# The expert gather reads x in place, with a step of eight elements, instead of a permuted copy

## The reference

```python
def hier_moe(x, w_grp, b_grp, w_exp, b_exp, w_gate, w_up, w_down):
    grp_logits = (xt @ w_grp).astype(jnp.float32) + b_grp
    ...
    weights = p_g[:, None] * jax.nn.softmax(top_vals, axis=-1)
    expert_id = g_top[:, None] * EXPERTS_PER_GROUP + top_idx
    ...
    def run_block(args):
        tok, e = args
        xb = x_pad[tok]
        h = jax.nn.silu(xb @ w_gate[e]) * (xb @ w_up[e])
        return h @ w_down[e]
    ...
    y = jnp.sum(y_assign.reshape(T, TOP_K, D).astype(jnp.float32) * weights[..., None], axis=1)
```

## Time and profile before

| | us |
|---|---|
| median of 3 runs | 1726.51 |
| lowest to highest | 1726.4 to 1727.92 |
| span of the profiled execution | 1725.1 |
| PE busy | 1413.4 (82%) |
| DVE busy | 375.8 (22%) |
| ACT busy | 269.0 (16%) |

### The profile page before, as it was taken

The page is one execution under the profiler, slowest core; times in us unless marked ns, Lnnn a source line. Parts: engine busy times, 40 slices in busy tenths (PEclk is TensorE's granted clock), DMA queues, the critical chain, the costliest instruction groups (busy, mean ns, idle before and its releaser), DMA issues.

```text
span 1725.1 us, 24051 instructions
## 1 busy us (share of the span) xinstructions
PE 1413.4 (82%) x9475; PEld 900.4 (52%) x9475; DVE 375.8 (22%) x752; ACT 269.0 (16%) x409; POOL 22.8 (1%) x79
## 2 busy tenths in 40 slices
PE   7999999877777777767999999997777777686785
PEld 3678886444434343433457788844443434343442
DVE  3222011511111111112433110114111111111134
ACT  1211000211111111111113200003111111121110
POOL 1000000000000000000000000000000000000000
PEclk9999999998989999989999999999899999898898
DMA  9532444389999999996844234334999999999970
GB/s 322 177 123 98 149 149 148 146 335 421 421 422 421 422 422 422 422 422 278 302 159 147 98 122 147 131 148 172 421 421 422 422 422 421 422 422 422 422 282 32
DMA packets 105010, 503.66 MB, mean 292 GB/s; under 512 B 15042, under 2 KB 18036, under 8 KB 54900
## 3 DMA queue, kind: packets, MB, share of 16 engines
q1 hardware_dynamic: 104228, 500.70, 72.4%
q10 hardware_dynamic: 720, 2.11, 0.3%
HBM read 501.73 MB, written 1.05 MB: 291 GB/s over the span
## 4 chain that ended last, share of the span: by engine, by line
PE 61%; DMA 29%; DVE 3%; ACT 3%; issue 2%; SPq 0%; POOL 0%; DVEq 0%; ACTq 0%; POOLq 0%
DMA ring<-in_w_down 29%; PE ps L552 16%; PE ps L979 10%; PE ps L861 7%; PE ps L839 5%; PE ps L989 5%; PE ps L566 5%; PE ps L957 4%; PE ps L944 4%; PE ps L588 2%; ACT scratch L1159 2%; PE ps L602 1%; DMA scratch<-in_ln 1%; DVE xT L1255 1%; DVE x L1205 0%
## 5 line engine op out<-in xcount | busy, mean ns | idle before, releaser
L957 PE MATMUL ps<-ring,scratch 128*32 128x256 f32 x4096 | 243.4, 391 | 69.3 <-DMA ring<-in_w_up 46.5
L552 PE MATMUL ps<-xT,ring 128*128 128x256 f32 x1280 | 279.7, 379 | 0.0
L552 PEld LDWEIGHTS ps<-xT,ring 128*128 128x128 f32 x1280 | 242.7, 190 | 33.7 <-issue 1.1
L979 PE MATMUL ps<-ring,scratch 128*32 128x512 f32 x1024 | 166.1, 807 | 108.5 <-DMA ring<-in_w_down 105.6
L957 PEld LDWEIGHTS ps<-ring,scratch 128*32 128x32 f32 x4096 | 156.7, 113 | 148.2 <-issue 77.5
L1594 DVE TENSOR_TENSOR scratch<-scratch,ps 128x1024 f32<-128x1024 f32 x64 | 78.1, 1221 | 405.0 <-PE ps L989 405.0
L979 PEld LDWEIGHTS ps<-ring,scratch 128*32 128x32 f32 x1024 | 44.2, 141 | 212.8 <-issue 212.8
L989 PE MATMUL ps<-scratch 128*128 128x512 f32 x256 | 118.4, 605 | 36.9 <-ACT scratch L1159 36.9
L944 PEld LDWEIGHTS ps<-scratch 128*128 128x128 f32 x1024 | 120.1, 193 | 15.9 <-issue 15.6
L944 PE MATMUL ps<-scratch 128*128 128x128 f32 x1024 | 120.1, 276 | 0.0
L989 PEld LDWEIGHTS ps<-scratch 128*128 128x128 f32 x256 | 46.0, 189 | 112.7 <-ACT scratch L1159 66.8
(11 more groups left out here) (247 smaller groups left out, 842.9 us busy)
## 6 DMA issues: line engine op xcount, KB each, us to landing
ring<-in_w_gate SPq DMA_DIRECT2D x128, 1024.0 KB, 13.9
ring<-in_w_up SPq DMA_DIRECT2D x128, 1024.0 KB, 18.3
ring<-in_w_down SPq DMA_DIRECT2D x128, 1024.0 KB, 16.7
ring<-in_w_in SPq DMA_DIRECT2D x48, 1024.0 KB, 6.9
ring<-in_w_br SPq DMA_DIRECT2D x12, 1024.0 KB, 6.0
ring<-in_w_o SPq DMA_DIRECT2D x8, 1024.0 KB, 4.9
ring<-in_w_ple_gate SPq DMA_DIRECT2D x8, 1024.0 KB, 8.1
ring<-in_ln SPq DMA_DIRECT2D x6, 1024.0 KB, 13.8
```

The costliest lines, as they stand in the source:

```text
L552: ins = mm(out[:, m * SEQ:m * SEQ + SEQ], w[k // per][:, k % per, m * 128:m * 128 + 128], rhs[:, k, :], start=(k == 0), stop=(k == nk - 1))
L957: ins = mm(ps[32 * j:32 * j + 32, 2, i * 256:i * 256 + 256], xgT[:, k, 32 * j:32 * j + 32], w[j][:, k, :], start=(k == 0), stop=(k == K - 1))
L979: ins = mm(ps[32 * j:32 * j + 32, 4 + n, :], hT[:, c, 32 * j:32 * j + 32], w[j][:, c, n * 512:n * 512 + 512], start=(c == 0), stop=(c == 1))
```

## The change

ACT no longer copies x into `xp`. The gather's stationary operand is a view of x with a step of eight elements, and PE waits for x itself (`xfinal`) where it waited for `xp_ready`. The area of `xp` stays reserved. The matrix product is the same in each element.

```diff
-                once(pe, "xp_ready", L)
+                pe.wait_ge(xfinal, 3 * L + 2)
                 once(pe, "yacc_zero", L)
...
-                            ins = mm(ps[:, k // 4, (k % 4) * 128:(k % 4) * 128 + 128], xp[:, t, k, :],
+                            ins = mm(ps[:, k // 4, (k % 4) * 128:(k % 4) * 128 + 128], x[:, t, :].rearrange("p (q k) -> p k q", k=K)[:, k, :],
                                      Psel[pb][:, t, :], start=(t == 0), stop=(t == T - 1))
...
-                act.wait_ge(xfinal, 3 * L + 2)
-                for t in range(T):
-                    ins = act.copy(xp[:, t, :, :], x[:, t, :].rearrange("p (q k) -> p k q", k=K))
-                ins.then_inc(ev["xp_ready"], 1)
                 copy_out("pu1", L, pus[:, 1, :, :].rearrange("p t n -> p (t n)"), pair("pu1"))
```

## The result

| | before | changed |
|---|---|---|
| median, us | 1726.45 | 1743.72 |
| lowest to highest, us | 1724.0 to 1727.92 | 1740.55 to 1746.65 |
| span of the profiled execution, us | 1725.1 | 1741.9 |

The ratio is 1.0105, with a 95% interval from 1.0091 to 1.012: the changed kernel is 1.05% slower, 17.3 us between the medians. The forecast was slower by 6.0 us, 1732.5 us. The measured time lies above the forecast's own range for its case, 1729 to 1740 us, and 1.3 us inside the end of the wide range, 1745 us.

A forecast was written before the change was run, and what follows sets the result against it. Expert weight streaming by DMA was taken to bound two plateaus, PE's path setting their start. -2.3 + 7.0 + 0.2 + 1.5 + 1.6 - 2 = +6.0 us on 1726.51 gave 1732.5 us; own range 1729 to 1740, wide range 1723.5 to 1745 us.

The forecast's parts named there:

- What goes: ACT's copy of x before the exponentials DVE waits for at L1507: 1.16 us saved per layer, -2.3 us.
- Price of a strided gather: PE's 32 fp32 weight loads per gather, step of 32 bytes: 3.5 us more a gather, bounds 3.0 to 4.0.
- The rule of two hits in a line: Trainium skill on SBUF: full-bandwidth reads need two hits per 16-byte line; a 32-byte fp32 step has one; no TensorE price.
- Rival B: At the gather, the step costs the weight load nothing; only the saving is left, 1724.2 us; chance 0.22.
- First gathers: First gather of each layer, on the path into the DMA plateau: 2 x 3.5 = +7.0 us.
- Layer 1, plateau and last group: PE's waits for weights absorb longer gathers inside the plateau, zero; the last group exceeds its waits by +0.2 us.
- Layer 2, plateau and last group: SP two slots behind, late down loads: three tight groups lose 0.5 us each, +1.5 us; last group +1.6 us.
- The slack of 3.0 us: Layer 2's tightest groups: time before the DMA queue runs dry, with 4.9 us from a load's issue to landing.
- Rival C: Load costing 4.5 us a gather; layer 2's short ring starves the DMA queue in every group; 1753 us, chance 0.10.
- A: The forecast's own case: 3.5 us more a gather, 1732.5 us, own range 1729 to 1740 us; chance 0.52.
- The clock: Longer gathers shorten PE's waits, so L979 and layer 2's first gather may keep full clock: -2 us, ends 0 and -5.
- Rivals D and E: D: half-idle array lowers the clock, L957's gate half slows, 1755 us, 0.06. E: load four times longer, about 1885 us, 0.10.

The follow-up runs named there:

- late_copy: Kernel before, gather still contiguous, ACT's copy of x moved after the last exponential that DVE waits for: 1724.2 us, ratio 0.9987.
- pad_part: Kernel before, contiguous gather and copy kept, 2.6 us of clock-keeping matmuls that nothing reads added ahead of each gather: 1737.33 us, ratio 1.0063.

## Why the forecast had the sign and missed the size

- **What goes**, -2.3 us: right. DVE's wait fell to 0.59 us in layer 1 (0.60 forecast), and late_copy, which has this part alone, has a ratio of 0.9987, 2.2 us.
- **Price of a strided gather**, 3.5 us: 3.91 us, inside its bounds of 3.0 to 4.0 and at ACT's end of them (0.97 ns an element; 3.91 us over 32 loads of 128 columns is 0.95 ns). It was carried over from ACT and DVE with no row of TensorE, so that it fitted is partly luck. The rule of two hits in a line held. Rival B fell.
- **First gathers**, +7.0 us: 2 x 3.91 = 7.8 us; the lower clock that layer 2's first gather had in the kernel before did not recur, which gave back 0.6 us there and 1.1 us in the clock-keeping matmuls before it.
- **Layer 1, plateau and last group**, 0 and +0.2 us: +0.3 us together. Right; the fourth group's L979 came 1.8 us late for the 1.7 forecast.
- **Layer 2, plateau and last group**, +1.5 and +1.6 us: 12.4 us together. This is the step that failed, by its size. The mechanism was named, the slots two behind and the third down load, but it was priced as a hard edge: only the excess over 3.0 us, only in the tightest group of four. Two things were wrong with it. The gather was 0.4 us longer than put in: with 3.91 us the same sum gives 3 x 0.9 us in the tight groups, 4 x 0.4 us in those with a slack of 3.5 us and 2.0 us in the last, 6.3 us together. The other 6 us come from the edge. The slack of 3.0 us was worked out with 4.9 us from issue to landing, the time of a load that finds the queue empty. In the changed kernel the third down loads from the second group on were issued 1.4 to 3.7 us before the load ahead of them landed, and they took 4.7 to 7.0 us; in the kernel before they were issued at least 5.4 us ahead, and each landed 2.5 to 2.6 us behind the one before it. So a load that is issued late can cost about 2 us more than the excess over the slack, and pad_part shows the beginning of it (1.8 us lost at 2.6 us of delay, 0.7 forecast). Why one such load takes 4.7 us and another 7.0 no run shows. Rival C had losses in most groups, 18 us in all for a gather longer by 4.5 us, and set its threshold at 3.5 to 4 us; with 3.91 us the kernel stood on it, and by the forecast's own sign, a DMA rate below 420 GB/s in most groups of layer 2, this is C's mechanism with A's gather. The sign of the forecast does not hang on the failed term: the first gathers alone outweigh the copy.
- **The clock**, -2 us: half right. Layer 2's first gather ran at full clock; but L979 stayed as slow as before (6.48 against 6.49 us in layer 1's third group, 6.32 against 6.27 us in layer 2's last but one), so the last groups got nothing back. Outside the terms of the sum, the clock differed between the two profiles by -3.0 us at the output projection and +2.1 us near the end; no run shows either to come from the change.
- Rivals D and E: the first groups' L957 ran 128 matmuls in 7.11 us as before, right behind a strided gather, so the half-empty array did not lower the clock; and the factor is two, not four.

## What to carry to other kernels

A stationary or moving fp32 operand with a step of four elements or more halved TensorE's reading rate here (233 ns a pair against 118); before one drops a permuting copy for it, one multiplies that by the number of times the operand is read, here 32 gathers against two copies, and looks for a place where the copy is hidden. A slack computed for a queue is not a hard edge: here loss began when 2.6 us were added against a computed 3.0. And where one resource ring serves two repetitions of a loop, compare the issue time of the same load in both: if it stands after a release in one and before it in the other, slots are being lost.

## What the runs showed of the hardware beyond this

- Step 3 in fp32 pays half the penalty of step 4 (173 ns between 118 and 233 ns).
- A copy of 1024 elements on ACT with the step pays the same factor of two, 2050 ns, and in the late place it takes 3.98 us for two beside DVE's work.
- In a stream of 1 MB loads at 420 GB/s, a load issued 5.4 us or more before the one ahead of it lands follows it in 2.5 to 2.6 us (third down loads of the kernel before, layer 2). Issued 1.4 to 3.7 us before (changed kernel), it follows in 2.5 to 4.6 us.
- Two slots of twelve are worth 4.7 us in a kernel whose plateau they don't slow, and 15.1 us in one whose plateau they do, 5.6 us of them before its second group.
